# The order of steps in the prompt mixing stage of a hybrid streaming encoder: a rule replaced by a written-out list for each engine

## The reference

```python
pr, pm, last = _project(x, shift_prev, w_in, mu_shift)    # LayerNorm'd rows @ w_in, token shift on the RWKV part
o_rw, state = _rwkv7(pr, state0, ...)                     # 8 heads x 64: S = S*w + sa (x) (kk*a) + v (x) k; y = S r
qn, qr = _mla_q(pm, ...); c, kr = _mla_latent(pm, ...)    # 8 heads, latent keys and values
kn, vv = _mla_expand(c, w_kvb)
o_at = _mla_prompt_attention(qn, qr, kn, kr, vv, cid)     # softmax attention, causal by chunks of 64
x = _post(x, _merge(o_rw, o_at, mla_out_g, w_out), ...)   # output projection, LayerNorm, squared-ReLU MLP, LayerNorm
```

## Time and profile before

| | us |
|---|---|
| median of 3 runs | 1880.21 (1875.96 to 1880.44) |
| the profiled execution | 1878.64 |
| its span, first to last instruction | 1876.9 |
| TensorE (PE) busy | 1735.7, 92% of the span |
| VectorE (DVE) busy | 1135.5, 61% |
| ScalarE (ACT) busy | 682.9, 36% |
| GpSimd (POOL) busy | 496.3, 26% |
| mean granted TensorE clock | 0.970 |

### The profile page before, as it was taken

The page is one execution under the profiler, slowest core; times in us unless marked ns, Lnnn a source line. Parts: engine busy times, 40 slices in busy tenths (PEclk is TensorE's granted clock), DMA queues, the critical chain, the costliest instruction groups (busy, mean ns, idle before and its releaser), DMA issues. The chain is left out here.

```text
span 1876.9 us, 41252 instructions
## 1 busy us (share of the span) xinstructions
PE 1735.7 (92%) x17079; PEld 1483.8 (79%) x17079; DVE 1135.5 (61%) x1885; ACT 682.9 (36%) x1483; POOL 496.3 (26%) x399
## 2 busy tenths in 40 slices
PE   5999997888899899898799997999999999999997
PEld 5899995566676676766677886999999988788886
DVE  7611024456756656646525579656666565889797
ACT  2222112344444545445333134222232344454443
POOL 0000002232323132221200001555555441436402
PEclk9999996899999999999899998999999999999999
DMA  5553230101110110111405341444444478567642
GB/s 195 191 194 99 71 99 27 53 32 58 50 65 16 64 49 17 49 64 38 129 26 186 113 151 51 135 130 130 130 130 135 151 271 278 195 215 252 220 131 100
DMA packets 158031, 219.96 MB, mean 117 GB/s; under 512 B 34470, under 2 KB 96574, under 8 KB 156824
## 3 DMA queue, kind: packets, MB, share of 16 engines
q1 hardware_dynamic: 156524, 212.62, 34.8%
q0 software_dynamic: 1328, 4.78, 0.7%
HBM read 152.75 MB, written 65.43 MB: 116 GB/s over the span
## 5 line engine op out<-in xcount | busy, mean ns | idle before, releaser
L1667 PE MATMUL c_p<-c_d_b_hi,c_d_a_hi 128*128 128x512 f32 x448 | 174.9, 390 | 1.9 <-DVE c_d_b_lo L1440 1.9
L1667 PE MATMUL c_p<-c_d_b_hi,c_d_a_lo 128*128 128x512 f32 x448 | 174.4, 389 | 0.0
L1667 PE MATMUL c_p<-c_d_b_lo,c_d_a_hi 128*128 128x512 f32 x448 | 174.4, 389 | 0.0
L1627 PE MATMUL c_p<-c_T_hi,c_up_op_hi 128*128 128x288 f32 x512 | 113.0, 300 | 12.1 <-DVE c_T_lo L1337 8.4
L1196 ACT ACTIVATE c_d_a_hi<-c_a_raw 128x512 fp32r<-128x512 f32 x112 | 70.3, 628 | 118.7 <-PE c_p L1667 104.9
L323 ACT ACTIVATE a_o<-a_pO 128x308 f32<-128x308 f32 (+1 forms) x80 | 32.6, 408 | 220.1 <-PE a_pO L462 205.6
L1627 PE MATMUL c_p<-c_T_lo,c_up_op_hi 128*128 128x288 f32 x512 | 112.5, 299 | 0.0
L1627 PE MATMUL c_p<-c_T_hi,c_up_op_lo 128*128 128x288 f32 x512 | 112.5, 299 | 0.0
L1434 DVE TENSOR_TENSOR c_d_a_lo<-c_a_raw,c_d_a_hi 128x512 fp32r<-128x512 f32 x112 | 89.3, 797 | 34.5 <-ACT c_d_a_hi L1196 34.1
L1333 DVE TENSOR_TENSOR c_up_op_lo<-c_up_raw,c_up_op_hi 128x512 fp32r<-128x512 f32 x80 | 90.4, 1135 | 25.4 <-ACT c_up_op_hi L1131 25.4
L462 PE MATMUL a_pO<-a_wh,a_hT_hi 128*128 128x308 f32 x576 | 95.5, 308 | 10.9 <-DVE a_hT_lo L390 10.5
(11 more groups left out here) (512 smaller groups left out, 4477.5 us busy)
## 6 DMA issues: line engine op xcount, KB each, us to landing
c_a_raw<-scratch_ops SPq DMA_DIRECT2D x112, 256.0 KB, 3.3
c_d_r<-w_down SPq DMA_DIRECT2D x96, 256.0 KB, 4.3
c_up_raw<-w_up SPq DMA_DIRECT2D x32, 512.0 KB, 5.4
scratch_ops<-c_hid SPq DMA_DIRECT2D x64, 256.0 KB, 2.7
scratch_ops<-c_h_sum SPq DMA_DIRECT2D x48, 256.0 KB, 2.0
scratch_p<-a_o SPq DMA_DIRECT2D x72, 154.0 KB, 1.8
m_pr<-w_in SPq DMA_DIRECT2D x8, 1232.0 KB, 8.2
m_pr<-scratch_p SPq DMA_DIRECT2D x8, 1232.0 KB, 5.3
```

The source lines that it names most:

```text
L1627: last = pe.matmul(pS[U.slot[j, m]][:, h, 0:PIECE], w[:, k, :], x[:, k, PIECE * h:PIECE * h + PIECE], start=m in (1, 2, 5) and k == 0 and ...
L1667: last = pe.matmul(bank, d_a[G.a_slot(a)][x][:, P * p:P * p + P], d_b[b % DB_RING][w][:, :], start=m in (1, 2, 5) and j == 0 and n == 0, s ...
```

## The change

`LATE` and the body of `schedule` go. A table `FULL_TILE` gives one list per engine, the same for each full tile, with each step's tile relative to i (1, 0, -1). Steps of tile 9, the sample tile, are left out by the same list as before. The instructions of a step aren't touched, and each engine issues the same set of steps as before. Steps for which an engine has no code are gone from its list.

```diff
-LATE = {True: ("mean", "keys", "latent_keys"), ...
+FULL_TILE = {
+    "tensor": (
+        ("score", 0, 0), ("grams", 0, None), ("weights", 0, 0), ("score", 0, 1), ("newton_t", 0, 0), ("grams_q", 0, None),
+        ("weights", 0, 1), ("newton_x", 0, 0), ("score", 0, 2), ("newton_t", 0, 1), ("values", 0, 0), ("weights", 0, 2),
+        ("newton_x", 0, 1), ("score", 0, 3), ("through", 0, None), ("turn_latent", 1, None), ("newton_t", 0, 2),
+        ("score", 0, 4), ("weights", 0, 3), ("newton_x", 0, 2), ("values", 0, 1), ("turn_lora", 1, None), ("newton_t", 0, 3),
+        ("lora_up", 1, None), ("weights", 0, 4), ("newton_x", 0, 3), ("score", 0, 5), ("newton_t", 0, 4), ("decay", 1, None),
+        ("weights", 0, 5), ("newton_x", 0, 4), ("score", 0, 6), ("values", 0, 2), ("latent_keys", 1, None), ("scan_z", 0, 0),
+        ("weights", 0, 6), ("score", 0, 7), ("scan_sa", 0, 0), ("scan_s", 0, 0), ("latent_rest", 1, None), ("scan_z", 0, 1),
...
+    "vector": (
...
+        ("shift_diff", 1, None), ("score", 0, 2), ("newton_t", 0, 1), ("norm", 1, None), ("score", 0, 3), ("mean", -1, None),
+        ("shift", 1, None), ("newton_t", 0, 2), ("variance", -1, None), ("score", 0, 4), ("newton_t", 0, 3),
...
+        ("keys", 1, None), ("latent_keys", 1, None), ("score", 0, 7), ("scan_sa", 0, 0), ("scan_s", 0, 0),
...
+    "scalar": (
+        ("score", 0, 0), ("squares", 1, None), ("weights", 0, 0), ("finish", -1, None), ("score", 0, 1), ("newton_x", 0, 0),
+        ("weights", 0, 1), ("score", 0, 2), ("newton_x", 0, 1), ("weights", 0, 2), ("score", 0, 3), ("turn_latent", 1, None),
+        ("mean", -1, None), ("weights", 0, 3), ("newton_x", 0, 2), ("lora", 1, None), ("turn_lora", 1, None),
+        ("score", 0, 4), ("lora_up", 1, None), ("newton_x", 0, 3), ("key_squares", 1, None), ("weights", 0, 4),
...
+    "pool": (
+        ("squares", 1, None), ("shift_diff", 1, None), ("variance", -1, None), ("lora_up", 1, None),
+        ("key_squares", 1, None), ("keys", 1, None), ("products", 1, None), ("latent_rest", 1, None), ("turn", 1, None),
+    ),
+}
...
     for i in range(1, count):
-        beside = ...
...
+        for name, ahead, v in FULL_TILE[engine]:
+            if ahead < 0 and i == 1:
+                continue
+            if i + ahead == count and name not in SAMPLE_AHEAD + ("squares", "shift_diff"):
+                continue
+            steps.append((name, i + ahead, v))
```

More of the change, by code:

```diff
@@ L1865 @@
 SAMPLE_AHEAD = ("shift", "norm", "lora", "turn_lora", "key_squares", "key_norm", "lora_up", "decay", "keys", "products")
-LATE = {True: ("mean", "keys", "latent_keys"),
-        False: ("shift", "norm", "turn_latent", "lora", "turn_lora", "key_squares", "key_norm", "keys", "latent_keys",
-                "products", "latent_rest", "gate_out", "finish")}
 def lead(engine):
@@ L1893, in lead @@
     return steps + second("turn_sides", "turn")
-def schedule(engine):
[L1902 to L1911, removed]
+FULL_TILE = {
[7 more added lines that the diff above has]
+        ("weights", 0, 6), ("score", 0, 7), ("scan_sa", 0, 0), ("scan_s", 0, 0), ("latent_rest", 1, None), ("scan_z", 0, 1),
+        ("weights", 0, 7), ("scan_sa", 0, 1), ("values", 0, 3), ("scan_s", 0, 1), ("merge_meta", 0, None),
+        ("turn_sides", 1, None), ("merge_out", 0, None), ("turn", 1, None), ("merge_turn", 0, None),
+    ),
+    "vector": (
+        ("score", 0, 0), ("grams", 0, None), ("score", 0, 1), ("newton_t", 0, 0), ("grams_q", 0, None),
+        ("shift_diff", 1, None), ("score", 0, 2), ("newton_t", 0, 1), ("norm", 1, None), ("score", 0, 3), ("mean", -1, None),
+        ("shift", 1, None), ("newton_t", 0, 2), ("variance", -1, None), ("score", 0, 4), ("newton_t", 0, 3),
+        ("gate_out", -1, None), ("score", 0, 5), ("newton_t", 0, 4), ("key_norm", 1, None), ("score", 0, 6),
+        ("keys", 1, None), ("latent_keys", 1, None), ("score", 0, 7), ("scan_sa", 0, 0), ("scan_s", 0, 0),
+        ("products", 1, None), ("scan_sa", 0, 1), ("scan_s", 0, 1), ("turn_sides", 1, None), ("turn", 1, None),
+        ("merge_turn", 0, None),
+    ),
+    "scalar": (
[3 more added lines that the diff above has]
+        ("score", 0, 4), ("lora_up", 1, None), ("newton_x", 0, 3), ("key_squares", 1, None), ("weights", 0, 4),
+        ("score", 0, 5), ("decay", 1, None), ("weights", 0, 5), ("newton_x", 0, 4), ("score", 0, 6), ("scan_z", 0, 0),
+        ("weights", 0, 6), ("score", 0, 7), ("scan_s", 0, 0), ("latent_rest", 1, None), ("scan_z", 0, 1), ("weights", 0, 7),
+        ("scan_s", 0, 1), ("merge_meta", 0, None), ("turn_sides", 1, None), ("merge_out", 0, None), ("turn", 1, None),
+    ),
+    "pool": (
+        ("squares", 1, None), ("shift_diff", 1, None), ("variance", -1, None), ("lora_up", 1, None),
+        ("key_squares", 1, None), ("keys", 1, None), ("products", 1, None), ("latent_rest", 1, None), ("turn", 1, None),
+    ),
+}
@@ L1912, in schedule @@
+def schedule(engine):
     count = len(TILES) - 1
-    ahead = lambda piece, i: [] if i > count else [(s, i, None) for s in piece if i < count or s in SAMPLE_AHEAD]
     steps = lead(engine)
     for i in range(1, count):
[L1917 to L1949, removed]
```

## The result

| | before | after |
|---|---|---|
| median of runs | 1880.01 us (9) | 1865.11 us (9) |
| ratio, 95% interval | | 0.9925 [0.9905, 0.9944] |
| profiled execution, its span | 1878.6, 1876.9 | 1864.5, 1862.7 |
| eight full tiles | 553.7 us | 535.1 us |
| TensorE idle in them | 57.0 us | 44.3 us |

The forecast was 1866, with the idle time falling from 57 to about 45 us. The ratio's interval lies wholly under 1: the kernel after is faster, by 0.6 to 1%. TensorE's busy time is less too, with the same instructions. Busy time by stretch of the kernel after (from:to, us, busy time of PE, weight loads, DVE, ACT, POOL, then granted clock, DMA share, GB/s): first stage, full tiles, rest, and tile 7.

A forecast was written before the change was run, and what follows sets the result against it. TensorE, with dependency gaps, was taken as the bound of the full tiles. 1878.6 less 12.0 us of gaps and 2 us of clock gave 1864.6 for the profiled execution, a median of 1866, range 1857 to 1877.

The forecast's parts named there:

- The bound and the gaps: Eight full tiles: TensorE bounds them, gains come only from gaps, idle falls from 57 to about 45 us.
- the sum: Gap savings over tiles 1 to 8, from 0 to 2.9 us each: 12.4 less 0.4 for key squares, 12.0 us.
- Level 0 to 1: Tile 4: early `score2` removes the 0.76 us gap; early `finish-` helps bring head 3's maximum 1.85 us earlier.
- Level 2: Tile 4: `score4` fills the 2.21 us gap behind the rotary key copy, leaving a 0.2 us wait.
- The new wait for F: TensorE ahead of `newton_x2`: a new gap of about 1.1 us, ended by VectorE's F, in tiles 2 to 6.
- the swap: VectorE does `shift+` (2.02 us) before `newton_t2`, costing a new 1.1 us wait ahead of `newton_x2` in tile 4.
- the slower case: Rival: the `shift+`/`newton_t2` swap delays F more than one score (1.05 us) past TensorE's readiness; 1886 us, chance 0.08.
- Level 3: Tile 4: VectorE, ending in `gate_out`, finishes last; `weights4` starts 1.5 us earlier, a 0.5 us gap stays.
- Key squares: ScalarE's `key_squares+` move gains nothing; queued `weights4` costs 0.1 us a tile, 0.4 us in all.
- Scan: `score7` ahead of `scan_sa0` fills a 0.67 us gap, adds about 0.55 us wait; net 0.
- Clock: Shorter gaps end some slow-clock stretches in the full tiles: 2 us gained.
- the whole 11 us: Lower-clock cost in the full tiles, 553.7 x 0.02; the skill's rule would return nearly all of it.

The follow-up runs named there:

- u_finish: Kernel after with `finish-` back behind `score2` on ScalarE: 1865.5 us, ratio to before 0.9924.
- u_shift: Kernel after with `newton_t2` ahead of `shift+` on VectorE again: 1862.3 us, ratio to before 0.9907.
- gate_shift: Kernel after with `newton_t2` ahead of `shift+` and `lora_up`'s wait for `gate_out` moved to ahead of the gate copy: 1855.7 us, ratio to before 0.9852.
- u_keysq: Kernel after with `key_squares+` and `weights4` back in their old places on ScalarE and GpSimd: 1862.9 us, ratio to before 0.9917.
- u_scan: Kernel after with `scan_sa0` ahead of `score7` again on TensorE and VectorE: 1866.7 us, ratio to before 0.9915.
- u_score4: Kernel after with `score4` back behind `values1` in TensorE's list: 1875.2 us, ratio to before 0.9972.
- only_s4: Kernel before with one edit, `score4` ahead of `weights3` on TensorE: 1874.4 us, ratio to before 0.9962.
- before_again: Kernel before profiled once more, unchanged, one run: 1889.1 us.
- after_again: Kernel after measured once more, unchanged: 1865.1 us, ratio to before 0.9909.
- u_values0: Kernel after with `values0` back ahead of `score2` and ScalarE's `weights` and `newton_x` steps in old order: 1868.4 us, ratio to before 0.9945.
- gate_only: Kernel after with only `lora_up`'s wait for `gate_out` moved to ahead of the gate copy: 1865.8 us, ratio to before 0.9910.
- only_pe: Kernel before with TensorE's list of after, except the scan's part; other engines as before: 1864.5 us, ratio to before 0.9912.

## Why the prediction was right

**The bound and the gaps: right.** Idle fell by 12.7 us where the sum said 12.0. By the undone parts, `score4` (6.3) and `values0` (4.7) carry it, `finish-` 2.8, the scan and the key squares nothing; these overlap and needn't add up. By tile the sum was less close: tile 8 gave 3.7 us where I had 2.0, and tile 3 gave 0.2 where I had 1.0. That the total came within 0.7 us is partly luck.

**Level 0 to 1: right.** `score2` follows `newton_x0`, the transposes of head 2 come without a gap, and `norm+` (L2671 after) has lost its 0.91 us for `finish-`. That `finish-` was worth as much as the rest of the level was my guess in `u_finish`, and was twice too high.

**Level 2: the places right, the sizes near.** I had 0.2 us left at the rotary key copy, under 0.5 as a sign; it is 0.56 (0.99 and 0.78 in tiles 2 and 3), and another 0.32 stands ahead of `score4`, since in tiles 3, 4 and 8 the exponential of head 3 isn't out yet (0.28, 0.32, 0.79 us). The new wait for F was put at 1.1 us; it is 1.49, 1.28, 1.06, 0.92 and 0.34 in tiles 2 to 6. I called it the cost of the swap. In idle time it is none: `u_shift` shows that without the swap as much is waited at the tanh. What I had not thought of is the low clock behind this wait in one or two of tiles 2 to 4. My condition for the slower case (F later than one score) looked at TensorE's arrival at `newton_x2`, and not at where both orders meet.

**Level 3: right about what ends last, wrong about where it is paid.** I expected 0.5 us to stay at `lora_up`; 0.21 stays, because TensorE has waited for F before (in tile 4 its slower matmuls behind that wait fill some of the gap too). That `gate_out` ends the stage is shown by `gate_shift`, which takes both waits away.

**Key squares: right.** ScalarE's `weights4` makes TensorE wait only in tiles 5 and 6 (0.51 and 0.29 us), and `u_keysq` finds no cost in the time. ScalarE's wait for GpSimd ahead of the square (L2564 after), which I gave as a sign, stands in no full tile: in tile 4 GpSimd's product is done by 586.41 and ScalarE comes to the square at 586.44, behind `newton_x3`.

**Scan: right.** About 0.55 us of new wait was forecast; there are 0.50 to 0.79 us a tile, and `u_scan` finds the trade even.

**Missed:** the wait for `m_c` at `turn_latent` went from 3.7 to 4.5 us (tile 3: 0.44 to 1.00). TensorE arrives earlier there and VectorE doesn't.

**Clock: the size right, the cause seen in part.** Over the 55 runs of before in the three sets of experiments the mean clock is 0.9654, over the nine of after 0.9679. The line through the 22 runs of before shared with the first four experiments falls by about 11 us per 0.01 of clock, so this is some 2.7 us of the 15; I had put 2. In the profiled pair the full tiles have 5.9 us less matmul time and the first stage is 5.5 us longer; that the forecast for the profiled execution, 1864.6, met 1864.5 so closely rests partly on these cancelling. Where the clock goes down most often, the last section shows: between the transposes of heads 3 and 4, the place of tile 7's 0.57 in the earlier trace rows. By the rule of the Trainium skill (TensorE: Matmul & The Clock Gate, "A second HAM failure mode: psum-queue depth-cycling"), as the prediction read it, nearly the whole 11 us would have come back; by the runs it didn't, for the full tiles still show 0.98. Its direction agrees: the profiles with the longer gap have more slow stretches there, 2, 4 and 5 against none to 2.

## What to carry to other kernels

When engines run fixed orders, find the join where two orders meet before pricing a swap: a wait that one removes reappears at the join, and here only moving the join (the wait for `gate_out`, together with the order of the two steps) saved more. Undo parts and compare the stage's idle time and the waits by place, not the medians alone. Read the clock of the stretch behind a gap as well, and don't take the clock out of a comparison when the change itself may move it. And look whether a wait stands ahead of more work than needs it.

## What the hardware showed that I had not expected

The spread of one kernel's runs is in good part a spread of the clock: about 11 us per 0.01 of mean clock for before, 11 to 16 for others. It isn't all: the profiled executions of `u_shift` and `u_finish` took 950.3 and 950.8 us behind the full tiles where the kernel after took 958.8, with the same code there. The first stage, with the same code in all, took 359.8 to 368.8 us in 14 profiles, at 0.92 to 0.94. Before had two of the shorter ones (363.3, 360.8); whether that is chance stays open.

The two kernels in which a gap of up to 2.2 us stands behind the rotary key copy ran at a mean clock of 0.965 (before, in three sets of runs: 0.9649 to 0.9658; `u_score4`: 0.9648); the ten with `score4` early ran at 0.967 to 0.971. `only_s4` differs from before in that one step, and its clock is 0.970. The stretch that is slowed lies behind the gap, from head 3's transposes to head 4's. Of the seven tiles from 2 to 8, those in which its clock is under 1.00:

| profile | slow tiles |
|---|---|
| before | 5 and 7 (0.83, 0.85) |
| before_again | 2 to 5 (0.81 to 0.83) |
| u_score4 | 2 to 5 and 8 (0.65 to 0.85) |
| the seven with `score4` early and `shift+` first (after, after_again, u_values0, u_scan, u_finish, u_keysq, gate_only) | one or two of tiles 2 to 4 (0.67 to 0.83) |
| the four with `score4` early and `newton_t2` first (u_shift, only_pe, only_s4, gate_shift) | none |

In `u_score4` the stretch holds the wait for F as well, so the two gaps can't be told apart there; in before it holds none. The gap alone doesn't decide it: tile 4's stretch ran at 1.00 in the first profile of before and at 0.82 in the second, with the same code. All profiles have low stretches elsewhere too, in tile 1 above all. Each kernel but before and after has a single profile, so how often a gap is followed by the lower clock stays open.
